# The delta stage's inverse in 32x32 diagonal blocks, and the second recurrence's small levels in 32-column tiles

## The reference, cut to what matters

```python
# gated delta rule, one direction, per chunk of c tokens
decay = exp(where(incl, gc[..., :, None] - gc[..., None, :], -inf))
a = where(strict, einsum('bhntd,bhnsd->bhnts', kb, k) * decay, 0.0)   # kb = k * beta
t_inv = triangular_solve(a + eye, eye, lower=True, unit_diagonal=True)
u = einsum('bhnts,bhnsv->bhntv', t_inv, v * beta[..., None])
...
v_new = u_n - einsum('bhtd,bhdv->bhtv', w_n, state)
o = einsum(qg_n, state) + einsum(qk_n, v_new)
state = state * gl_n[..., None, None] + einsum('bhsd,bhsv->bhdv', kd_n, v_new)

# HGRN2 (the second recurrence), one direction
dec = exp(where(incl, b_n[:, :, :, None, :] - b_n[:, :, None, :, :], -inf))
att = einsum('bhtd,bhsd,bhtsd->bhts', q_n, k_n, dec)
o = einsum(q_n * exp(b_n), state) + einsum('bhts,bhsv->bhtv', att, i_n)
state = state * exp(last)[..., None] + einsum(k_n * exp(last - b_n), i_n)
```

## Time and profile before

| | us |
|---|---|
| median of 3 runs | 2887.77 (2886.1 to 2888.53) |
| span of the profiled execution, first to last instruction | 2890.9 |
| TensorE busy / weight loads | 2788.4 / 2285.6 |
| DVE busy | 1511.7 |
| ACT busy | 1206.3 |
| POOL busy | 879.3 |

### The profile page before, as it was taken

One profiled execution on the slowest core, in us unless ns is written; L12 is line 12 of the kernel. 1 busy time (PEld: TensorE's weight loads), 2 busy tenths in 40 slices (PEclk: granted clock), 3 DMA queues, 4 the chain that ended last, 5 costly groups with the idle time before them and its releaser, 6 DMA issues. The chain is left out here.

```text
span 2890.9 us, 41563 instructions
## 1 busy us (share of the span) xinstructions
PE 2788.4 (96%) x17106; PEld 2285.6 (79%) x17106; DVE 1511.7 (52%) x2145; ACT 1206.3 (42%) x1933; POOL 879.3 (30%) x476
## 2 busy tenths in 40 slices
PE   8999998999999999999989999999999999999999
PEld 6787876888888877878768888888787778888887
DVE  7565566347626465655663476165786553631120
ACT  5653665233213245536652333132444553342231
POOL 2353020014544423530200145344001324344433
PEclk9999999999999999999999999999999999999999
DMA  5102202433423331022023333233422223333322
GB/s 174 56 3 77 68 2 74 109 110 95 117 73 98 99 89 59 3 72 73 2 74 103 110 96 116 79 98 100 106 81 73 64 64 101 93 95 95 98 84 80
DMA packets 414558, 235.86 MB, mean 82 GB/s; under 512 B 24244, under 2 KB 404770, under 8 KB 413730
## 3 DMA queue, kind: packets, MB, share of 16 engines
q1 hardware_dynamic: 413490, 233.18, 28.0%
q10 hardware_dynamic: 880, 0.02, 0.0%
HBM read 226.88 MB, written 6.29 MB: 81 GB/s over the span
## 5 line engine op out<-in xcount | busy, mean ns | idle before, releaser
L2318 POOL TENSOR_TENSOR WLO<-RAW,WHI 128x1024 fp32r<-128x1024 f32 (+1 forms) x199 | 521.8, 2628 | 979.0 <-ACT WHI L2154 979.0
L146 PE MATMUL PS<-HHI,WHI 128*128 128x512 f32 x2016 | 796.6, 395 | 5.5 <-DVE WLO L3050 2.2
L148 PE MATMUL PS<-HHI,WLO 128*128 128x512 f32 x2016 | 787.4, 391 | 0.0
L147 PE MATMUL PS<-HLO,WHI 128*128 128x512 f32 x2016 | 787.1, 390 | 0.0
L146 PEld LDWEIGHTS PS<-HHI,WHI 128*128 128x128 f32 x2016 | 380.5, 189 | 98.1 <-issue 7.9
L147 PEld LDWEIGHTS PS<-HLO,WHI 128*128 128x128 f32 x2016 | 380.6, 189 | 80.9 <-issue 3.2
L148 PEld LDWEIGHTS PS<-HHI,WLO 128*128 128x128 f32 x2016 | 379.9, 188 | 79.6
L2154 ACT CAST WHI<-RAW 128x1024 fp32r<-128x1024 f32 (+1 forms) x202 | 221.5, 1100 | 510.1 <-PE PS L148 496.4
L2307 DVE TENSOR_TENSOR X<-X,PS 128x512 f32<-128x512 f32 x48 | 33.0, 688 | 334.1 <-PE PS L148 334.1
L3112 POOL TENSOR_TENSOR WLO<-RAW,WHI 128x1280 fp32r<-128x1280 f32 x31 | 91.3, 2947 | 319.3 <-ACT WHI L2995 319.3
L2290 DVE SCALAR_TENSOR_TENSOR ACC<-GP,PARS,ACC 128x512 f32<-128x512 f32 x88 | 163.1, 1853 | 3.1
(11 more groups left out here) (489 smaller groups left out, 4913.2 us busy)
## 6 DMA issues: line engine op xcount, KB each, us to landing
RAW<-in_w_up SPq DMA_DIRECT2D x88, 512.0 KB, 3.8
RAW<-in_w_mlp SPq DMA_DIRECT2D x64, 512.0 KB, 3.8
RAW<-in_w_in SPq DMA_DIRECT2D x46, 512.0 KB, 4.0
RAW<-in_w_down SPq DMA_DIRECT2D x32, 704.0 KB, 4.4
RAW<-in_w_in SPq DMA_DIRECT2D x20, 1024.0 KB, 5.2
RAW<-in_w_gate SPq DMA_DIRECT2D x32, 512.0 KB, 3.9
RAWQ<-in_w_in SPq DMA_DIRECT2D x24, 512.0 KB, 3.9
RAW<-in_w_out SPq DMA_DIRECT2D x24, 512.0 KB, 4.8
```

Of the source, the lines that this page charges most:

```text
L146: e.matmul(out, wh, xh, start=first and n == 0, stop=False)
L147: e.matmul(out, wh, xl, start=False, stop=False)
L148: last = e.matmul(out, wl, xh, start=False, stop=final and n == len(quads) - 1)
L2318: pool.tensor_tensor(slot(WLO, u), source(u), slot(WHI, u), ALU.subtract).then_inc(lo_s, 1)
```

## The change

In the delta stage T, TT, LB and PP hold the four 32x32 diagonal blocks instead (128 rows of 32 columns a head). Levels 1 to 4 are 16 matmuls of 32x32 a lane for each P and D, instead of 8 of 64x64. Level 5 is no more a level of the same kind: its P takes the block of AT that lies off the diagonal of a 64x64 block, its D makes the block of the inverse (into another bank of PSUM), in both forms that are needed. T is not transposed on TensorE any more: ACT copies TT's blocks straight into TTF (`keep_diagonal`), and the level-5 blocks of TTF and of a new buffer TQ (the first half of T, as the corner's P needs it) are written by ACT (`keep_below`) and DVE (`first_half`, `below_first_half`). AT now holds 128 columns a head: the 64x64 diagonal block and the corner, in one buffer (ATQ is gone), cut out by five DVE instructions instead of three and scaled by one set of ACT instructions of 128 columns instead of two. `last_p` doesn't wait for the state any more, `last_d` does. POOL's sixth mask goes.

In the second recurrence the diagonal and levels 0 to 4 are 16 matmuls a lane with 32x32 results instead of 8 with 64x64. Level 5 is 8 matmuls (32x32), and its result is copied by ACT into AT without a mask; DVE's gather of level 5 goes, the others are half as wide, and DVE places the four 32x32 diagonal blocks into AT (`blocks_placed`), so that the outputs wait for one more semaphore.

The diff, cut to its core:

```diff
-    CH, W, L = 4, 64, LEVELS - 2
+    CH, W, V, L = 4, 64, 32, LEVELS - 2
     HALVES = (slice(0, W), slice(W, P))
     FIRST, SECOND = HALVES, HALVES[::-1]
+    QUARTERS = [slice(V * q, V * q + V) for q in range(4)]
+    EARLY, LATE = (QUARTERS[0::2], QUARTERS[1::2]), (QUARTERS[1::2], QUARTERS[0::2])
+    DIAG, OFF = (slice(0, V), slice(V, W)), (slice(V, W), slice(0, V))
+    FIRST_EARLY, FIRST_LATE = (QUARTERS[0], QUARTERS[3]), (QUARTERS[1], QUARTERS[2])
...
     def level_p(m, d, n):
-        pe.wait_ge(S["lb"][d], m * (L + 1) + n + 1)
+        b = B[d]
+        pe.wait_ge(S["lb"][d], m * L + min(n + 1, L))
         if n == 1:
             pe.wait_ge(S["tc"][d], m * L + 1)
-            if m:
-                pe.wait_ge(S["t"][d], m * L)
         else:
             pe.wait_ge(S["t"][d], m * L + n - 1)
         for h in H4:
-            for rows in HALVES:
-                last = pe.matmul(small(d, 0, 0)[rows, h, :], B[d]["LB"][rows, n % 2, h, :], B[d]["T"][rows, m % 2, h, :], start=True, stop=True)
+            if n < L:
+                for rows in QUARTERS:
+                    last = pe.matmul(quarter(d, 0)[rows, h, :], b["LB"][rows, n % 2, h, :], b["T"][rows, m % 2, h, :], start=True, stop=True)
+            else:
+                for one, two in zip(EARLY[d], LATE[d]):
+                    last = pe.matmul(quarter(d, 0)[two, h, :], b["AT"][one, m % 2, h, OFF[d]], b["T"][one, m % 2, h, :], start=True, stop=True)
         last.then_inc(S["p"][d], 1)
 
     def level_d(m, d, n):
         pe.wait_ge(S["pc"][d], m * L + n)
         pe.wait_ge(S["tc"][d], m * L + n)
+        b = B[d]
+        if n == L:
+            pe.wait_ge(S["aq"][d], min(m + 2, CH))
+            if m:
+                pe.wait_ge(S["tcd"][d], m)
         for h in H4:
-            for rows in HALVES:
-                last = pe.matmul(small(d, 0, 1)[rows, h, :], B[d]["TT"][rows, m % 2, h, :], B[d]["PP"][rows, h, :], start=True, stop=True)
+            if n < L:
+                for rows in QUARTERS:
+                    last = pe.matmul(quarter(d, 1)[rows, h, :], b["TT"][rows, m % 2, h, :], b["PP"][rows, h, :], start=True, stop=True)
+            else:
+                for one, two in zip(EARLY[d], LATE[d]):
+                    pe.matmul(below(d)[one, h, :], b["PP"][two, h, :], b["TT"][two, m % 2, h, :], start=True, stop=True)
+                two = FIRST_LATE[d]
+                last = pe.matmul(below(d)[two, h, :], b["TT"][two, m % 2, h, :], b["PP"][two, h, :], start=True, stop=True)
         last.then_inc(S["dd"][d], 1)
 
     def last_p(m):
         for d in lanes:
             pe.wait_ge(S["t"][d], m * L + L)
-            pe.wait_ge(S["aqb"][d], m + 1)
-            pe.wait_ge(S["aq"][d], min(m + 2, CH))
+            pe.wait_ge(S["atb"][d], m + 1)
+            pe.wait_ge(S["off"][d], m + 1)
+        for h in H4:
+            for d in lanes:
+                one, two = FIRST[d], SECOND[d]
+                last = pe.matmul(small(d, 1, 1)[two, h, :], B[d]["AT"][one, m % 2, h, W:], TQ[one, h, :], start=True, stop=True)
+                if h == 3:
+                    last.then_inc(S["p6"][d], 1)
+
+    def last_d(m):
+        for d in lanes:
+            pe.wait_ge(S["tcd"][d], m + 1)
+            pe.wait_ge(S["ttd"][d], m + 1)
+            pe.wait_ge(S["off"][d], m + 1)
             if m:
                 pe.wait_ge(S["su"][d], m)
...
     def times_beta(m, d):
-        act.wait_ge(S["at"][d], m + 1)
+        act.wait_ge(S["aq"][d], m + 1)
         for h in H4:
             part = B[d]["AT"][:, m % 2, h, :]
             last = act.activation(part, part, ACT.Copy, scale=beta_of(chunk(m, d), d, h))
         last.then_inc(S["atb"][d], 1)
 
-    def corner_times_beta(m, d):
-        one = FIRST[d]
-        act.wait_ge(S["aq"][d], m + 1)
-        for h in H4:
-            part = ATQ[one, m % 2, h, :]
-            last = act.activation(part, part, ACT.Copy, scale=beta_of(chunk(m, d), d, h)[one])
-        last.then_inc(S["aqb"][d], 1)
-
...
+    def keep_diagonal(m, d):
+        act.wait_ge(S["tc"][d], m * L + L)
+        if m:
+            act.wait_ge(S["vn"][d], m)
+        else:
+            act.wait_ge(S["mk"][0], 5)
+        for rows in QUARTERS:
+            last = act.copy(B[d]["TTF"][rows, :, rows], B[d]["TT"][rows, m % 2])
+        last.then_inc(S["ttd"][d], 1)
+
+    def keep_below(m, d):
+        act.wait_ge(S["dd"][d], m * L + L)
+        for one, two in zip(EARLY[d], LATE[d]):
+            last = act.activation(B[d]["TTF"][one, :, two], below(d)[one], ACT.Copy, scale=-1.0)
+        last.then_inc(S["off"][d], 1)
 
     def keep_last(m, d):
         act.wait_ge(S["p6"][d], m + 1)
-        if m:
-            act.wait_ge(S["vn"][d], m)
-        for rows in HALVES:
-            act.copy(B[d]["TTF"][rows, :, rows], small(d, 3, 0)[rows])
         act.copy(PQ[SECOND[d]], small(d, 1, 1)[SECOND[d]]).then_inc(S["tcd"][d], 1)
...
     def decayed_keys(m, d):
-        b, one, two = B[d], FIRST[d], SECOND[d]
+        b, two = B[d], SECOND[d]
         dve.wait_ge(S["e"][d], m + 1)
         dve.wait_ge(S["kk"][d], m + 1)
+        if m == 0:
+            dve.wait_ge(S["mk"][1], 1)
         if m > 1:
-            dve.wait_ge(S["lb"][d], (m - 1) * (L + 1))
+            dve.wait_ge(S["lb"][d], (m - 1) * L)
+            dve.wait_ge(S["p"][d], (m - 1) * L)
             dve.wait_ge(S["p6"][d], m - 1)
         raw = per_head(bank(d, 1))
-        for rows in HALVES:
-            last = dve.tensor_tensor(b["AT"][rows, m % 2], raw[rows, :, rows], b["DM"][rows, m % 2, :, rows], ALU.mult)
-        last.then_inc(S["at"][d], 1)
-        dve.tensor_tensor(ATQ[one, m % 2], raw[one, :, two], b["DM"][one, m % 2, :, two], ALU.mult).then_inc(S["aq"][d], 1)
+        for one, rows in zip(EARLY[d], HALVES):
+            dve.tensor_tensor(b["AT"][one, m % 2, :, 0:W], raw[one, :, rows], b["DM"][one, m % 2, :, rows], ALU.mult)
+        for rows in LATE[d]:
+            dve.tensor_tensor(b["AT"][rows, m % 2, :, DIAG[d]], raw[rows, :, rows], b["DM"][rows, m % 2, :, rows], ALU.mult)
+        dve.tensor_tensor(b["AT"][:, m % 2, :, W:], raw[:, :, two], b["DM"][:, m % 2, :, two], ALU.mult).then_inc(S["aq"][d], 1)
 
     def level(m, d, n):
         b = B[d]
         dve.wait_ge(S["dd"][d], m * L + n)
-        dve.tensor_tensor(b["T"][:, m % 2], b["T"][:, m % 2], small(d, 0, 1), ALU.subtract).then_inc(S["t"][d], 1)
-        if n < L:
-            dve.wait_ge(S["t"][d], m * L + n)
-            dve.transpose(row(b["TT"][:, m % 2]), row(b["T"][:, m % 2])).then_inc(S["tc"][d], 1)
+        dve.tensor_tensor(b["T"][:, m % 2], b["T"][:, m % 2], quarter(d, 1), ALU.subtract).then_inc(S["t"][d], 1)
+        dve.wait_ge(S["t"][d], m * L + n)
+        dve.transpose(row(b["TT"][:, m % 2]), row(b["T"][:, m % 2])).then_inc(S["tc"][d], 1)
+
+    def first_half(m, d):
+        if m:
+            dve.wait_ge(S["p6"][d], m)
+        dve.wait_ge(S["t"][d], m * L + L - 1)
+        one, two = FIRST_EARLY[d], FIRST_LATE[d]
+        for rows in (one, two):
+            dve.tensor_copy(TQ[rows, :, within(rows)], B[d]["T"][rows, m % 2])
+
+    def below_first_half(m, d):
+        one, two = FIRST_EARLY[d], FIRST_LATE[d]
+        dve.wait_ge(S["dd"][d], m * L + L)
+        dve.tensor_scalar(TQ[two, :, within(one)], below(d)[two], -1.0, None, ALU.mult).then_inc(S["t"][d], 1)
...
         for h in H4:
-            for rows in HALVES:
-                last = pe.matmul(small(d, n)[rows, h, :], x[:, h, rows], x[:, h, rows], start=True, stop=True)
+            if n < SMALL_LEVELS:
+                for rows in QUARTERS:
+                    last = pe.matmul(small(d, n)[rows, h, :], x[:, h, rows], x[:, h, rows], start=True, stop=True)
+            else:
+                for one, two in zip(early_quarters[d], late_quarters[d]):
+                    last = pe.matmul(small(d, n)[one, h, :], x[:, h, one], x[:, h, two], start=True, stop=True)
         last.then_inc(S["a"][d], 1)
...
     def outputs(m, d):
         b = B[d]
+        pe.wait_ge(S["as"][d], m + 1)
         pe.wait_ge(S["af"][d], m + 1)
...
     def assembled(m):
         for d in lanes:
-            act.wait_ge(S["mk"][0], 3)
-            act.wait_ge(S["ac"][d], (m + 1) * (LEVELS - 1))
+            act.wait_ge(S["a"][d], m * LEVELS + LEVELS - 1)
             if m:
                 act.wait_ge(S["o"][d], m)
-            for rows in HALVES:
-                act.copy(B[d]["AT"][rows, :, rows], B[d]["AC"][rows])
+            else:
+                act.wait_ge(S["mk"][0], 5)
+            for one, two in zip(early_quarters[d], late_quarters[d]):
+                act.copy(B[d]["AT"][one, :, two], small(d, LEVELS - 2)[one])
         for d in lanes:
             one, two = FIRST[d], SECOND[d]
             act.wait_ge(S["a"][d], (m + 1) * LEVELS)
-            act.copy(B[d]["AT"][one, :, two], small(d, LEVELS - 1)[one]).then_inc(S["af"][d], 1)
+            act.copy(B[d]["AT"][one, :, two], small(d, LEVELS - 1, W)[one]).then_inc(S["af"][d], 1)
...
+    def blocks_placed(m, d):
```

(45 more changed lines are left out.)

75 lines of the change are left out of this document (39 added, 36 removed).

## The result

The changed kernel takes 2867.7 us (median of 4 runs, 2865.4 to 2872.7) against 2886.9 of the kernel before on the same chip: ratio 0.9935, 95% interval 0.9924 to 0.9947. That is 19 us faster, inside the range of the prediction but less than half of its 40 us; the likeliest case alone (2836 to 2860) doesn't hold it. The profiled span is 2868.0 us against 2890.9.

The account below looks back on a forecast made before the run. It took the delta stage as bound by the rate of TensorE's small matmuls. Two layers of 11.2 (delta) and 9.9 us (HGRN) made 42 off 2890.9: 2848.9, 2846 in the runs' terms, plus 2 given back: 2848, range 2834 to 2880.

Parts of the forecast that it names:

- the likeliest case alone: Whole kernel, if the forecast rather than any rival holds: 2836 to 2860 us; the forecast was given 0.57.
- The unit: A group: one P or D step of a level, both lanes, on TensorE; from 1.08 us to 0.75.
- rival 1: TensorE's groups: a tile needs 58 ns however narrow, so a group saves nothing; 16 us saved in all, 2872; chance 0.17.
- rival 2: TensorE's queue: 57 ns a matmul, 1.98 us a group, +31 a layer, 2950; chance 0.14 for any cost over 35 ns.
- new holes behind ACT of over 1 us a chunk: TensorE's timeline: such holes, or four-tile groups that do not get faster, would make the prediction wrong.
- written the saving off: Delta middle chunk: P4, D4, P5, D5 save 1.3 us on paper; outputs wait for ACT's scaled values, only 0.35 is left.
- HGRN: The second recurrence: middle chunks 2.4 us shorter each, the last 2.7, 9.9 a layer.
- the sum's last line: Whole kernel: 2 us given back for queue effects, from 2846 in the runs' terms to 2848.
- rival 4: First delta chunk: a later first P could leave TensorE at 1.2 GHz longer; some 2 us a layer, no chance given.
- the first delta chunk: Latencies count: +1.3 us before the first LB, five levels some 3 shorter, 0.5 given back; 1.4 saved, bounds -1 to +3.
- nothing now: Delta middle chunk: ACT's added diagonal and below-part copies cost nothing beside state and outputs; 1 us a chunk without that cover.
- the prediction's best end: Whole kernel: 0.62 us a group and no queue effects, 2 x 27 = 54 us saved, 2834.

Follow-up runs that it names:

- experiments 4, 6 and 7: 4: changed kernel with ScalarE's order in the delta stage changed, 2861.9 us; 6 and 7: that plus one-column matmuls moving the borders of 256, 2859.9 and 2876.9 us.
- fillers: Extra matmuls in TensorE's delta-stage waits: on the changed kernel 2871.3 us; large ones with ScalarE's new order 2876.2; smaller, with moved borders 2860.0, with earlier queries too 2856.1.
- the stuffed waits: Kernel before, with four waits on a long-reached semaphore ahead of each 64x64 matmul of delta levels 1 to 4: 3035.5 us, ratio 1.0507.

## Why the prediction was wrong

**The unit was right, a little timid.** 0.75 us forecast, 0.69 measured; neither a floor in the tile (rival 1) nor 2 us (rival 2 in its first form). 64 records start in 0.69 us, 11 ns apart over four tiles. The trace disagrees with the 25 ns between starts of the Trainium skill (TensorE: Matmul & The Clock Gate, "Wait — 56ns, not 53.3ns?") where it is taken over tiles. (Rival 2's +31 a layer is 0.9 x 42 - 8 = 30 by its own terms; nothing hangs on it.)

**The delta chunks went as worked out.** Middle: 2.5 saved by forecast, 2.56 measured. P1 with the corner 1.37 and 1.43. The outputs behind ScalarE at +7.5 us from the key products: 203.86 to 211.32 is 7.46. The 1.09 us wait for ScalarE ahead of them is the sign that the prediction named for being wrong ("new holes behind ACT of over 1 us a chunk"), but it lies where the prediction had already written the saving off. Last chunk: P, queries and D of the corner forecast 3.29, measured 3.20 (242.43 to 245.63), and both waits of the earlier trace rows are gone:

```profile
242.43 0.68 PE L910 MATMUL PS<-TQ,AT 64*64 64x64 f32 x16
243.04 2.05 PE L864 MATMUL PS<-QKV 128*128 128x128 f32 x16
245.02 0.68 PE L926 MATMUL PS<-TTF,PQ 64*64 64x64 f32 x16
```

**HGRN gave more.** Middle chunk forecast 23.2 us, measured 22.8 (1404.00 to 1426.79, with a hole of 0.6 in it). Last chunk, to the end: 24.3 before, 22.5 after in layer 2 with two holes of 4.2 us in sum in it; no wait for ScalarE is left before its outputs (0.3 forecast).

**The step that failed is the sum's last line:** "For queue effects that a walk passes over I give back 2". In its place the trace has 21 us of pauses over 0.5 us in the four stages, and moving the borders alone moved the time by 17.0 us. The prediction asked how fast TensorE's queue can start instructions, took the answer from stretches of 26 records, and never asked how fast the program reaches the queue. The count was in front of it: 3456 more records, four instructions a matmul, and rival 2 even spoke of the doubled count, but as a price on every matmul. What came is a price on blocks, zero at most borders and 0.5 to 2.7 us at 18 of them.

**The second is rival 4,** put at "some 2 us a layer": low clock went from 31 to 78 us, some 14 us by the rate above. Holes and longer waits come before most of those stretches (432.92 to 434.64 before the one at 435.3), so part of this is the first cause again; how much stays open.

**The third is the first delta chunk,** forecast 1.4 shorter and measured 3.3 and 1.2 longer. Of the terms, +1.3 us to the first P was 1.4 and 1.3. The rest is holes (2.4 and 0.6 us), 12.7 and 7.7 us more at the low clock (3.8 and 2.3 by the rate above), and the wait of the corner's P for ScalarE (0.5 and 1.7); they overlap, since their sum is more than the miss. The last was given as "nothing now", with state and outputs as cover, and the first chunk has neither.

**How much each of the two cost stays open.** The four stages are 21.1 us shorter, where 42 was forecast. If the holes (23 us of any length) and the added low clock (14 by the rate) counted in full, the change would otherwise have given 58, HGRN 17 a layer and delta 12. That is more than the 54 of the prediction's best end, whose group took 0.62 us and not 0.69. So the two are too high together: a hole can lie where a wait would have stood anyway. The kernels of experiments 4, 6 and 7 have the same code but for the borders. A fit to their 12 stage times, with a constant for each of the four stages, gives some 0.45 us lost for each us of hole and 0.36 for each us of low clock. That is an estimate that misses single stages by up to 1.2 us; by it the holes cost 10 us here and the clock 17. Either way the two cover the miss. But the second comes in part from the first, and no run here held the clock without fillers.

## What to carry to other kernels

When a change multiplies the small instructions of an engine, price the program as well as the work: divide the added instructions by the size of a block (256 here) and look for stretches where a block goes in less time than one takes to arrive (some 3.5 us here). A step that is "covered" in the middle of a pipeline has to be looked at again in its first and last turn, where the cover is missing. And where an engine's queue holds an output back, try its order before giving the gain up: two such edits were worth 6 and 4 to 5 us.

## What the runs showed of the hardware that I had not expected

- TensorE's instructions are fetched during the run in blocks of 256 (16 KB). In the 11 profiled kernels that have 32x32 groups, 169 of 173 pauses of over 0.5 us without a semaphore in the four stages stand ahead of an instruction of remainder 193 or 194 of the count; the other 4 are among or beside the fillers. Before, and with the stuffed waits, there are none.
- A border mostly costs nothing if the block before it took over 3.5 us (45 of 609 have a hole); if it took less, about half have one (124 of 261). The line is sharper with a block's time taken from the end of the hole before it: then 162 of 259 quick blocks end in a hole, and 7 of 611 slow ones. When packets leave 3.1 to 3.4 us late the hole is 2.2 to 2.7 us at the same pace (last HGRN chunk). What delays them I did not settle.
- A wait on a semaphore that was reached long ago costs TensorE some 0.07 us when it is an instruction of its own between matmuls (2048 more such records, 3035.5 - 2889.9 = 145.6 us). Some of this is the clock, which was low for 137 us of the two delta stages there (17 before); in the lane shown, at full clock, 16 such records add 1.39 us, 0.09 each.
